# Product of gelu and routing weight on VectorE instead of GpSimd, coefficients in eights, in the expert stage of a streaming encoder layer

## What is computed

```python
def block(args):
    xb, ib, wb = args
    ub = jnp.take(u_exp, ib, axis=0)
    act = jax.nn.gelu(jnp.einsum('nhed,nd->nhe', ub, xb).astype(jnp.float32), approximate=False)
    vb = jnp.take(v_exp, ib, axis=0)
    return jnp.einsum('nhe,nhed->nd', wb * act, vb.astype(jnp.float32))
```

## Time and profile before

| | us |
|---|---|
| median of 3 runs | 6347.76 (6342.45 to 6349.72) |
| the profiled execution | 6345.53 |
| its span | 6343.9 |

### The profile page before, as it was taken

The page is one execution under the profiler, slowest core; times in us unless marked ns, Lnnn a source line. Parts: engine busy times, 40 slices in busy tenths (PEclk is TensorE's granted clock), DMA queues, the critical chain, the costliest instruction groups (busy, mean ns, idle before and its releaser), DMA issues. The chain is left out here.

```text
span 6343.9 us, 64313 instructions
## 1 busy us (share of the span) xinstructions
PE 5213.5 (82%) x22820; PEld 4087.2 (64%) x22820; DVE 3630.7 (57%) x4027; ACT 1561.3 (25%) x1834; POOL 2077.5 (33%) x1538
## 2 busy tenths in 40 slices
PE   6767999999997887988677105999999788888885
PEld 2224788888886534867256105999999666666664
DVE  5642221113674233321321694888877799999998
ACT  4433312222222111111111101333322222232222
POOL 0000000000000231000000276788888655555553
PEclk9976999999998997989578557999999999999998
DMA  7742233233322455331233327999999999999997
GB/s 257 255 147 74 85 106 98 87 104 104 113 97 100 149 184 177 134 120 63 99 121 117 121 7 247 400 390 390 389 373 371 369 394 392 392 394 391 393 392 292
DMA packets 499757, 1409.60 MB, mean 222 GB/s; under 512 B 98269, under 2 KB 188343, under 8 KB 426825
## 3 DMA queue, kind: packets, MB, share of 16 engines
q1 hardware_dynamic: 317630, 737.27, 32.6%
q0 software_dynamic: 154960, 630.43, 26.8%
q10 hardware_dynamic: 27072, 40.91, 1.8%
HBM read 1265.04 MB, written 144.49 MB: 222 GB/s over the span
## 5 line engine op out<-in xcount | busy, mean ns | idle before, releaser
L219 DVE TENSOR_TENSOR w_lo<-w_stage,w_hi 128x2048 fp32r<-128x2048 f32 x248 | 568.0, 2290 | 1500.1 <-ACT w_hi L215 1498.2
L224 PE MATMUL ps<-w_hi,act_hi 128*128 128x512 f32 x3040 | 1196.4, 394 | 49.7 <-DVE act_lo L1013 23.0
L225 PE MATMUL ps<-w_lo,act_hi 128*128 128x512 f32 x3040 | 1190.8, 392 | 0.0
L226 PE MATMUL ps<-w_hi,act_lo 128*128 128x512 f32 x3040 | 1189.9, 391 | 0.0
L215 ACT ACTIVATE w_hi<-w_stage 128x2048 fp32r<-128x2048 f32 x248 | 474.8, 1915 | 1587.2 <-PE ps L226 1491.4
L1447 POOL DMA_INDIRECT d_wT<-wt_all,put_all x384 | 745.6, 1942 | 291.4 <-DVEq L1562 136.8
L1902 DVE SCALAR_TENSOR_TENSOR acc<-v_ring,coef,acc 128x2048 f32<-128x2048 f32 x254 | 799.6, 3148 | 36.6 <-DMA v_ring<-v_exp,idx_all 28.4
L1782 PE MATMUL ps<-act_hi,x_hi 128*128 128x384 f32 x2048 | 689.5, 337 | 145.8 <-DVE x_lo L1907 145.1
L1782 PE MATMUL ps<-x_hi,cx_hi 128*128 128x512 f32 x1536 | 616.3, 401 | 220.4 <-DVE cx_lo L1912 179.3
L1854 ACT ACTIVATE x_hi<-x_stage 128x1024 fp32r<-128x1024 f32 x512 | 540.9, 1056 | 926.0 <-PE ps L1784 494.9
L1907 DVE TENSOR_TENSOR x_lo<-x_stage,x_hi 128x1024 fp32r<-128x1024 f32 x512 | 626.4, 1223 | 196.6 <-ACT x_hi L1854 174.2
(11 more groups left out here) (240 smaller groups left out, 5671.0 us busy)
## 6 DMA issues: line engine op xcount, KB each, us to landing
x_stage<-u_turned SPq DMA_DIRECT2D x256, 512.0 KB
x_stage<-v_exp SPq DMA_DIRECT2D x256, 512.0 KB
w_stage<-w_ada SPq DMA_DIRECT2D x96, 1024.0 KB, 5.1
w_stage<-w_in SPq DMA_DIRECT2D x96, 1024.0 KB, 5.2
gw<-d_g SPq DMA_DIRECT2D x256, 192.0 KB
gw<-d_wT SPq DMA_DIRECT2D x256, 192.0 KB
d_wT<-zero SPq DMA_DIRECT2D x12, 2048.0 KB, 28.8
d_g<-gob ACTq DMA_DIRECT2D x128, 192.0 KB
```

The lines of the kernel that those rows point to most:

```text
L219: dve.tensor_tensor(w_lo[:, q % 2], w_in_st[:, q], w_hi[:, q % 2].bitcast(F32), ALU.subtract).then_inc(w_split, 1)
L224: pe.matmul(out, lhs[0], rhs[0], start=first, stop=False)
L225: pe.matmul(out, lhs[0], rhs[1], start=False, stop=False)
L226: return pe.matmul(out, lhs[1], rhs[0], start=False, stop=last)
```

## The change

`weigh` leaves POOL's program and stands in DVE's: three products after x_lo of n = NU, then one in each n from NU + 1 to N - 3 (for m = n - NU + 2), right behind cx_lo, on whose `clo_done` it waits. NB goes from 4 to 8, LAG from 6 to 10; ACT's gelu for the gathered slots is set to the new NB.

```diff
-    LAG = 6
+    LAG = 10
     DEPTH = 4
     RING = 4
-    NB = 4
+    NB = 8
...
-            def weigh(m):
-                pool.wait_ge(gw_in[m % 4], 32 * (m // 4 + 1))
-                if m >= 3:
-                    pool.wait_ge(clo_done, m - 2)
-                pool.tensor_tensor(gob[:, m % 3], gw[:, m % 4, 0], gw[:, m % 4, 1], ALU.mult).then_inc(c_done, 1)
-
...
-                if s == NKEY:
-                    for m in range(3):
-                        weigh(m)
-                elif s > NKEY:
-                    for m in (2 * (s - NKEY) + 1, 2 * (s - NKEY) + 2):
-                        if m < NV:
-                            weigh(m)
...
-                if n >= 10 and (n - 10) % 8 == 0 and (n - 10) // 8 < NS // NB:
-                    b = (n - 10) // 8
+                if n >= 2 * NB + 2 and (n - 2 * NB - 2) % (2 * NB) == 0 and (n - 2 * NB - 2) // (2 * NB) < NS // NB - 1:
+                    b = (n - 2 * NB - 2) // (2 * NB)
...
+            def weigh(m):
+                dve.wait_ge(gw_in[m % 4], 32 * (m // 4 + 1))
+                if m >= 3:
+                    dve.wait_ge(clo_done, m - 2)
+                dve.tensor_tensor(gob[:, m % 3], gw[:, m % 4, 0], gw[:, m % 4, 1], ALU.mult).then_inc(c_done, 1)
+
             for n in range(N):
                 dve.wait_ge(hi_done, n + 1)
                 dve.tensor_tensor(w_lo[:, n % DEPTH], stg[:, n % 3], w_hi[:, n % DEPTH].bitcast(F32),
                                   ALU.subtract).then_inc(lo_done, 1)
+                if n == NU:
+                    for m in range(3):
+                        weigh(m)
                 m = n - NU - 1
                 if m >= 0:
                     dve.wait_ge(chi_done, m + 1)
                     dve.tensor_tensor(c_lo[:, m % DEPTH], gob[:, m % 3], c_hi[:, m % DEPTH].bitcast(F32),
                                       ALU.subtract).then_inc(clo_done, 1)
+                    if n < N - 2:
+                        weigh(n - NU + 2)
```

## The result

The changed kernel takes 6383.12 us at the median of 7 runs (6370.02 to 6386.33), the kernel before 6349.77 (7 runs, 6342.45 to 6366.00). The medians are 33 us apart and the means 25 us; the ratio, which goes by the means, is 1.0039, 95% interval 1.0024 to 1.0054. So the change made the kernel slower by some 25 us, where 38 us less were forecast. The profiled execution of the changed kernel has a span of 6381.6 us, 37.7 more than that of before.

The account below looks back on a forecast made before the run. PE was taken to bound the first half, DVE the second, with DMA engines next. 123 slots at 9.65 for 10.04 us (-48), +3.7, +11 and -4.4 gave -38 us: 6310 us, range 6269 to 6362.

Parts of the forecast that it names:

- Step 1: Second half, DVE: with POOL's two products gone, DVE gains 2.26 us a slot, 2.34 for a coef slot.
- Step 2: Second half, DVE: two products of 128x384 with their waits add 0.60 us for each n, 1.20 a slot.
- Steps 3 and 4: Second half, DVE: coef in eights saves 0.03 us a slot; DVE's slot becomes 8.9 us (8.6 to 9.7) against 10.04.
- Step 5: Second half: the DMA engines, moving 3.93 MB a slot, set the pace at 9.65 us, so only 0.39 us is kept.
- The slice method: DMA rate read in 2.5 us slices of one slot: 405, 420, 407 and 314 GB/s, slack in the last.
- Step 6: Second half, loads of gw: issue-to-landing time L of 8.3 to 9.3 us makes a slot at least 8.9 to 9.9.
- The rival "the lead of gw sets the pace": Second half: L grows, at L = 10.0 the slot is 10.6 us, total about 6427 us; chance 0.10.
- The rival "the DMA engines are full already": Second half: no DMA room, the slot stays at 9.9 to 10.04 us, total 6341 to 6365 us; chance 0.20.
- Step 7: Seam of the halves: the wait for gw now stands ahead of more DVE work, +3.7 us (0 to 6).
- Step 8: End of the kernel: LAG 10 for 6 leaves four more additions behind the last n, +11 us.
- Step 9: Last four slots, without a gather of u: DVE's 8.9 us holds there, -4.4 us.
- The rule against the change: DMA in the second half: a skill page's limit of about 358 GB/s leaves no room, slot stays at 10.04 us.

Follow-up runs that it names:

- the half pair on POOL: Kernel before, products on POOL, with the gelu half of each pair gw not loaded and the product squaring the dense weight: 6312.2 us in one run.
- the earlier pairs: Changed kernel with the pairs gw asked for one n earlier, same bytes and waits: 6296.24 us, ratio 0.9910 to the kernel before.
- the runs with more lead: Changed kernel with pairs gw asked for one n earlier (ratio 0.9910; with LAG 6, NB 4 0.9904), or issued ahead of the stage load (0.9909).

## Why the prediction was wrong, step by step

- **Step 1 (the stretch goes): right.** 2.35 us for each accumulation, and the half pair on POOL shows the same relation from the other side: DVE loses what POOL's products last.
- **Step 2 (+0.60 us for each n): right in kind, 0.66 measured.** cx_lo 5503.08, product 5503.73, dot product 5504.21: 0.65 with the wait and 0.48.
- **Steps 3 and 4 (8.9 us for DVE): 9.04.**
- **Step 5 (the DMA engines set the pace at 9.65 us): the size was right, 9.50 at 416 GB/s, but only where the lead allowed it.** The slice method read the room rightly: 405 to 420 in full slices, 416 in the end. It was taken for the bound, and wasn't. The rate of 396 in the changed kernel is an effect of DVE waiting.
- **Step 6 (the lead of gw) is the step that failed.** Its formula holds in kind: a slot can't be shorter than L and a constant, 0.3 us in the rows above (9.01 - 8.7) and up to 0.6. Its L of 8.3 to 9.3 was right too, 8.9 at the median. What failed is what was made of them. A lower bound of 8.9 to 9.9 "just beside the 9.65 taken" was let pass as if the smaller number didn't count. But DVE works in order and has no reserve: a pair that lands late (10.97 us in the rows above) costs its whole delay, one that lands early gives nothing back, as DVE's own 9.04 holds then. The period is the mean of the larger of the two in each step, not the larger of the means: 9.04 plus 1.0 of waits, with slots from 9.0 to over 11 us. Why one pair takes 8 us to land and another over 10 no run shows. The rival "the lead of gw sets the pace" is what happened. It was priced at L = 10.0 for every pair, 10.6 us and 6427, and thereby looked rare (0.10); with the spread of L it stands at 10.0 to 10.2 us, where nothing is gained, and that needed no unusual L.
- **The rival "the DMA engines are full already"** has the right period and the wrong reason. The DMA share doesn't tell them apart, being 1.01 in both kernels; the earlier pairs did. The rate in slices gives a hint once one knows what to compare it with: 350 to 421 GB/s where DVE's waits hold it back, 413 to 422 in 35 of 40 slices where it is freed.
- **Step 7 (the seam, +3.7, 0 to 6): +5.7.** Its own terms give less than it said: 5000.52 + 1.4 + 2.2 + 1.1 is 5005.2 and not 5005.8, so +3.1. Short by the second and third pair, which weren't there when the first was (1.94 us of wait in the row of 5025.47, and 0.44 before the third product).
- **Step 8 (LAG, +11): +11.3, right**, and 12 with LAG and NB alone.
- **Step 9:** right in kind. The last two dot products start 8.3 us apart in the changed kernel (6290.01 and 6298.35) and 10.2 in the one before (6262.14 and 6272.35). But the last four, 28.9 us from first to last, gain only 1.4 us on 30.3, since one slot among them lasts 11.5 us; -4.4 was forecast.
- **The sum:** the 48 us of the period did not come (some 3 us in one profile; the second has 10.19 against 10.04, 19 us the other way). Seam and end cost 17 us, where 14.7 were forecast, and 17 to 36 us are ratios of 1.0027 to 1.0057, around the 1.0039 measured. The profile's other 22 us (+29.6 in the first half, -7.1 ahead of it) belong for the most part to the executions, which the forecast, made against one profile, had no term for.
- **The rule against the change** said 358 GB/s for a core between HBM and SBUF (the Trainium skill, "DMA: Bandwidth & Descriptors", "Where 436 GB/s comes from"). The trace reaches 416 GB/s over 300 us with one core at work, close to the 425 that the same page of the Trainium skill has for a core alone. Its case for "no room" is refuted here.

## What to carry to other kernels

When work moves to an engine that runs in order, ask for each transfer that it now waits for how far ahead it was issued, in steps of that engine's own program, and compare this lead with the longer landings under load, not with the median: late ones cost in full and early ones give nothing back. A DMA share of 1.0 is no proof of a bandwidth limit, since it stood at 1.01 here while waits held the rate back; a run with the same bytes and one step more lead tells them apart. And one profile against one profile carries the difference of two executions, here 30 us in a half that the change hardly touches.

## What the runs showed of the hardware

- A two-input DVE instruction beside POOL's two products lasts longer by about the time of these products: 2.26 us for 2.00, 1.88 for 1.61. It hits even a 128x4 product (0.14 us alone, 2.48 beside them). With gathers alone on POOL the accumulation stays at 2.35 us.
- A POOL product of 128x384 takes 1.0 us from two tiles and 0.8 from one read twice; on DVE it takes 0.56.
- The DMA engines of this core gave 416 GB/s over 300 us with pieces of 1.5, 4 and 8 KB in a row, and no slice of 12.5 us from 5100 to 5600 us gave more than 424 in the kernel before, the changed one or the runs with more lead.
- The pace of back-to-back matmuls of 384 columns in the first half was 173, 174 or 176 ns (300 us by the count) in three profiles at a granted clock of 1.00, two of them of the same program. No run here says what it depends on.
